# A two-layer hybrid encoder on one Trainium2 core: program unrolled, stages meeting by token halves, five weight slots, norm roots on ScalarE, new mixer order

## The reference

```python
def rms_norm(x, g):
    y = xf * lax.rsqrt(jnp.mean(xf * xf, axis=-1, keepdims=True) + EPS)
    return (y * g.astype(jnp.float32)).astype(x.dtype)

def swiglu(h, w_gate, w_up, w_down):
    return (jax.nn.silu(h @ w_gate) * (h @ w_up)) @ w_down

for l in range(DEPTH):
    h = swiglu(rms_norm(x, ffn1_norm_pre[l]), ffn1_w_gate[l], ffn1_w_up[l], ffn1_w_down[l])
    x = x + 0.5 * rms_norm(h, ffn1_norm_post[l])
    proj = rms_norm(x, mix_norm_pre[l]) @ w_in[l]
    lru_x, lru_g, sq, sk, sv, dq, dk, dv = jnp.split(proj, list(IN_OFFSETS), axis=-1)
    y = jnp.concatenate([y_lru, y_swa, y_diff], axis=-1) @ w_out[l]
    x = x + rms_norm(y, mix_norm_post[l])
    h = swiglu(rms_norm(x, ffn2_norm_pre[l]), ffn2_w_gate[l], ffn2_w_up[l], ffn2_w_down[l])
    x = x + 0.5 * rms_norm(h, ffn2_norm_post[l])
```

## Time and profile before

| | us |
|---|---|
| median of 3 runs | 1081.08 (1079.9 to 1083.06) |
| profiled execution, its own time | 1079.87 |
| its span in the trace | 1078.1 |
| TensorE busy | 1001.6 (93%) |
| VectorE busy | 703.5 (65%) |
| ScalarE busy | 511.8 (47%) |
| GpSimd busy | 112.6 (10%) |
| mean granted TensorE clock | 0.967 |

### The profile page before, as it was taken

The page is one execution under the profiler, slowest core; times in us unless marked ns, Lnnn a source line. Parts: engine busy times, 40 slices in busy tenths (PEclk is TensorE's granted clock), DMA queues, the critical chain, the costliest instruction groups (busy, mean ns, idle before and its releaser), DMA issues. The chain is left out here.

```text
span 1078.1 us, 15592 instructions
## 1 busy us (share of the span) xinstructions
PE 1001.6 (93%) x5486; PEld 865.2 (80%) x5486; DVE 703.5 (65%) x895; ACT 511.8 (47%) x646; POOL 112.6 (10%) x84
## 2 busy tenths in 40 slices
PE   7999999699994999999879999996999959999996
PEld 6888888588984888888768888885889758888885
DVE  6765556757778666556677655667577776655655
ACT  5444444345563544444354444443456535444442
POOL 5000000304004000000130000003130130000000
PEclk9999999889997999999989999998999969999998
DMA  8767656423342556556355655563342525565550
GB/s 235 251 212 263 194 178 232 135 90 127 136 147 88 159 192 195 188 191 209 116 139 194 195 190 191 172 226 117 117 138 100 167 75 187 193 195 177 177 171 40
DMA packets 131246, 180.57 MB, mean 167 GB/s; under 512 B 4112, under 2 KB 114840, under 8 KB 131200
## 3 DMA queue, kind: packets, MB, share of 16 engines
q1 hardware_dynamic: 128944, 176.24, 49.7%
q0 software_dynamic: 2256, 3.76, 1.7%
HBM read 178.92 MB, written 2.63 MB: 168 GB/s over the span
## 5 line engine op out<-in xcount | busy, mean ns | idle before, releaser
L458 PE MATMUL UP<-xT,whi 128*128 128x512 f32 x1648 | 582.6, 398 | 4.9 <-DVE xT L1052 4.9
L997 DVE TENSOR_TENSOR wlo<-raw,whi 128x2048 fp32r<-128x2048 f32 (+1 forms) x156 | 355.3, 2280 | 185.7 <-ACT whi L739 185.5
L460 PE MATMUL UP<-xT,wlo 128*128 128x256 f32 x1648 | 461.9, 280 | 0.0
L458 PEld LDWEIGHTS UP<-xT,whi 128*128 128x128 f32 x1648 | 309.4, 188 | 80.6 <-issue 6.3
L739 ACT ACTIVATE whi<-raw 128x2048 fp32r<-128x2048 f32 x162 | 306.0, 1891 | 131.2 <-PE Y L481 125.2
L460 PEld LDWEIGHTS UP<-xT,wlo 128*128 128x128 f32 x1648 | 311.2, 189 | 1.4
L481 PE MATMUL Y<-whi,hidT 128*128 128x512 f32 x640 | 178.9, 391 | 0.0
L481 PEld LDWEIGHTS Y<-whi,hidT 128*128 128x128 f32 x640 | 117.4, 188 | 24.6
L506 PE MATMUL UP<-ident 128*128 128x128 f32 x276 | 50.5, 357 | 54.1 <-DVE x L1070 29.3
L481 PE MATMUL Y<-wlo,hidT 128*128 128x512 f32 x320 | 99.5, 392 | 0.0
L506 PEld LDWEIGHTS UP<-ident 128*128 128x128 f32 x276 | 47.4, 265 | 58.3 <-DVE x L1070 30.7
(11 more groups left out here) (182 smaller groups left out, 828.8 us busy)
## 6 DMA issues: line engine op xcount, KB each, us to landing
raw<-in_ffn_w_gate SPq DMA_DIRECT2D x44, 1024.0 KB, 5.4
raw<-in_ffn_w_up SPq DMA_DIRECT2D x44, 1024.0 KB, 5.4
raw<-in_ffn_w_down SPq DMA_DIRECT2D x44, 1024.0 KB, 4.8
raw<-in_w_in SPq DMA_DIRECT2D x20, 1024.0 KB, 5.1
raw<-in_w_out SPq DMA_DIRECT2D x6, 1024.0 KB, 4.8
gains<-in_ffn_norm_pre SPq DMA_DIRECT2D x4, 512.0 KB, 4.8
gains<-in_ffn_norm_post SPq DMA_DIRECT2D x4, 512.0 KB, 5.4
raw<-in_w_out SPq DMA_DIRECT2D x4, 512.0 KB, 3.6
```

The costliest lines, as they stand in the source:

```text
L458: nc.tensor.matmul(dst[:, 0:2 * S], h[:, kt, c:c + P], xT[:, kt, :, :].rearrange("p h s -> p (h s)"), start=kt == 0, stop=False, skip_grou ...
L460: mm = nc.tensor.matmul(dst[:, S:2 * S], o[:, kt, c:c + P], xT[:, kt, 0, :], start=False, stop=kt == KT - 1, skip_group_check=True)
L997: V.tensor_tensor(wlo[:, slot, 0:n], raw[:, slot, 0:n], whi[:, slot, 0:n].bitcast(F32), ALU.subtract).then_inc(lo_ready, 1)
```

## The change

The whole program is unrolled: no loops on any engine.

*Ring.* Five slots. `wlo` is laid over `raw`, so the low part of a unit is written in place over what was loaded. A unit is loaded when PE has used the unit five before (`unit_used`), and split at the same condition. All weight splits are on ACT and DVE.

*Feed-forward order.* The down unit of pair i follows the up unit of pair i + 2 (`LAG`), and the last three down units stand at the end (`TAIL`): first their token half 0, then their half 1. Hidden values lie in four places of `yT`.

*Stage boundary.* Norms, additions and transposes go by token half `t` and feature half `h`. DVE does `post` and `pre` for half 0 and then for half 1, POOL none of it. The root of a norm is an ACT square root (`norm_root`) followed by a reciprocal and one refinement on DVE (`norm_scale`); `load_root_table` calls Sqrt once at the end of each feed-forward stage. PE turns the first quarter of the next stage before the last six matmuls of a feed-forward stage (after them in a mixer), and begins the next stage with two units in which tokens are rows (`token_units`): for both units the products with the high part of `x`, then those with the low part, first for half 0 and then for half 1. They are gate and up of pair 0, whose hidden values are turned by four more transposes, or in a mixer the two value units. Between the halves PE runs 3 + 3 identity matmuls.

*Mixer.* Order new, four output units of two row blocks each instead of three such and two single ones; the two value units first, window attention last of the three jobs.

*Start and end.* The first `x` half is loaded first; the 28 identity matmuls before the first transposes are gone. The output is stored in four pieces.

The core of the diff:

```diff
-RING = 3
...
+RING = 5
...
+for pair_ in range(PAIRS):
+    FFN_ORDER += [("gate", pair_), ("up", pair_)]
+    if LAG <= pair_ < PAIRS - 1:
+        FFN_ORDER.append(("down", pair_ - LAG))
+TAIL = tuple(range(PAIRS - 1 - LAG, PAIRS))
+FFN_ORDER += [("down", pair_) for pair_ in TAIL]
...
+        wlo = nc.alloc_sbuf_tensor_at("wlo", [P, RING, 2048], F32R, offset=ring_base)
         whi = sb("whi", [P, RING, 2048], F32R)
-        wlo = sb("wlo", [P, RING, 2048], F32R)
...
+                if k >= RING:
+                    sp.wait_ge(unit_used, k - RING + 1)
+                sp.dma_start(dst, src).then_inc(raw_loaded[k % RING], 16)
...
-                split(l, FFN2_0)
-                add_first(l * 3 + 1)
-                weigh_first(l * 3 + 2)
...
-            def turn_x(stage):
-                for t in range(NT):
-                    pe.wait_ge(x_ready[t], stage + 1)
-                    keep_clock(4)
-                pe.wait_ge(x_squared, stage * 3 + 3)
-                keep_clock(6)
-                for h, t in TURN_ORDER:
-                    if h == 0:
-                        pe.wait_ge(xs_ready[t], stage + 1)
...
+            def turn(s, t, h):
+                pe.wait_ge(xs_ready, quarter(s, t, h) + 1)
+                for kt in range(4 * h, 4 * h + 4):
+                    tr = nc.tensor.transpose(UP[:, 1024 * t + P * kt:1024 * t + P * kt + P],
+                                             xs[:, t, kt * P:(kt + 1) * P], ident[:, :])
+                tr.then_inc(xs_turned, 1)
...
+            def token_units(s, t, first_signal):
+                units = stage_unit(s, 0), stage_unit(s, 1)
+                tok = slice(t * P, t * P + P)
+                for n, k in enumerate(units):
+                    unit_ready(k)
+                    for kt in range(KT):
+                        if n == 0 and kt % 4 == 0:
+                            pe.wait_ge(xT_hi, quarter(s, t, kt // 4) + 1)
+                        dst = bank(Y, 2 * t + n, 0, UC)
+                        nc.tensor.matmul(dst, xT[:, kt, 0, tok], cols(k, whi)[:, kt, :], start=kt == 0, stop=False)
+                        nc.tensor.matmul(dst, xT[:, kt, 0, tok], cols(k, wlo)[:, kt, :], start=False, stop=False)
+                for n, k in enumerate(units):
+                    for kt in range(KT):
+                        if n == 0 and kt % 4 == 0:
+                            pe.wait_ge(xT_lo, quarter(s, t, kt // 4) + 1)
+                        mm = nc.tensor.matmul(bank(Y, 2 * t + n, 0, UC), xT[:, kt, 1, tok], cols(k, whi)[:, kt, :],
+                                              start=False, stop=kt == KT - 1)
+                    mm.then_inc(unit_used if t else first_signal, 1)
+            def enter(s, first_signal, turned_parts):
+                for h in range(turned_parts, 2):
+                    turn(s, 0, h)
+                token_units(s, 0, first_signal)
+                if s:
+                    pe.wait_ge(x_half, quarter(s - 1, 1, 0) + 1)
+                    keep_clock(3)
+                    pe.wait_ge(x_squared, quarter(s, 1, 1) + 1)
+                    keep_clock(3)
+                for h in range(2):
+                    turn(s, 1, h)
+                token_units(s, 1, first_signal)
...
+                        for b in range(2):
+                            token_rows(k, hidden_parts(i), 0, b, False, True).then_inc(y_banks, 1)
+                for i in TAIL:
+                    k = ffn_unit(s, "down", i)
+                    if i < TAIL[-1]:
+                        both_banks(k, hidden_parts(i), 1).then_inc(unit_used, 1)
+                    else:
+                        token_rows(k, hidden_parts(i), 1, 0, False, True).then_inc(y_banks, 1)
+                        if s + 1 < STAGES:
+                            turn(s + 1, 0, 0)
+                        token_rows(k, hidden_parts(i), 1, 1, False, True).then_inc(unit_used, 1)
...
+            def norm_root(s, t, kind):
...
+                A.activation(root[:, t, kind:kind + 1], ss[:, t, kind, 1:2], ACT.Sqrt, scale=1.0 / (D * factor * factor),
+                             bias=base_sum[:, t, kind:kind + 1]).then_inc(root_ready, 1)
...
+            def load_root_table():
+                act.wait_ge(eps_set, 1)
+                A.activation(nw[:, 3, 3:4], epsb[:, :], ACT.Sqrt)
...
+                for t in range(NT):
+                    if s:
+                        square_y(s, t, 0)
+                        if t:
+                            turned_hi(s, 0, 1)
+                        square_y(s, t, 1)
+                        norm_root(s, t, POST)
+                        if t == 0:
+                            for k in splits:
+                                split(k)
+                    for h in range(2):
+                        square_x(s, t, h)
...
+                V.scalar_tensor_tensor(half, ss[:, t, kind, 1:2], -0.5 / (D * factor * factor), half_sum[:, t, kind, 0:1], ALU.mult, ALU.add)
+                dve.wait_ge(root_ready, root_number(s, t, kind) + 1)
+                link(V.reciprocal(y, root[:, t, kind:kind + 1]))
+                link(V.scalar_tensor_tensor(w, y, half, y, ALU.mult, ALU.mult))
+                link(V.scalar_tensor_tensor(y, w, 1.5, y, ALU.add, ALU.mult))
...
+            def post(s, t, between=lambda: None):
+                weigh_y(s, t, 0)
+                norm_base(s, t, POST)
...
+                weigh_y(s, t, 1)
+                norm_scale(s, t, POST)
+                for h in range(2):
+                    add_y(s, t, h)
+            def pre(s, t):
+                norm_base(s, t, PRE)
+                norm_scale(s, t, PRE)
+                for h in range(2):
+                    weigh_x(s, t, h)
+            def enter(s, splits):
+                if s:
+                    post(s, 0)
+                    for k in splits:
+                        split(k)
+                    pre(s, 0)
+                    post(s, 1, lambda: turned_lo(s, 0, 0))
+                    turned_lo(s, 0, 1)
+                    pre(s, 1)
...
+                in_tile(U_SWKV, 0)
+                turn_output(l, JOB_A)
+                in_tile(U_SWKV, 1)
+                pe.wait_ge(mix_lo, l * OUT_UNITS + 1)
+                turn_weights(l, JOB_B)
+                scores(l, JOB_SWA)
+                in_tile(U_LRU_G, 0)
+                values(l, JOB_B)
+                lru_gate(l, 0)
+                in_tile(U_LRU_G, 1)
+                lru_gate(l, 1)
...
+                both_banks(out_unit(OUT_A), mixed(OUT_A), 0, True)
+                wait_tile_read(pe, l, U_LRU_G, 1)
+                turn_output(l, JOB_B)
...
+                job_output(JOB_A)
+                tile(U_SWQ, 1)
+                softmax_weights(JOB_B)
+                tile(U_SWKV, 0)
+                job_lo(JOB_A, 1)
+                sp(11)
+                softmax_logits(JOB_SWA)
+                tile(U_LRU_G, 0)
+                sp(12)
+                job_output(JOB_B)
+                tile(U_LRU_G, 1)
+                softmax_weights(JOB_SWA)
+                recurrence_inputs()
+                job_lo(JOB_B, 2)
```

More of the change, by code:

```diff
@@ L974, in _ @@
[L974 to L985 removed]
+                A.activation(sm[:, 8, 0:2], sm[:, 7, 0:2], ACT.Exp, scale=-1.0)
@@ new lines, in small_parameters @@
+                A.activation(sm[:, 0, 4:6], sm[:, 0, 0:2], ACT.Exp).then_inc(sp_exp, 1)
+            load_root_table()
+            for s in range(STAGES):
+                enter(s, [stage_unit(s, 1)] if s and s % 3 != 2 else [])
+                if s % 3 == 1:
+                    mixer(s)
+                else:
+                    ffn(s)
+            for t in range(NT):
+                for b in range(2):
+                    square_y(STAGES, t, b)
+                norm_root(STAGES, t, POST)
@@ L1367, in shape_constants @@
+            for t in range(NT):
+                post(STAGES, t)
 def shape_constants():
```

1540 lines of the change are left out of this document (762 added, 778 removed).

## The result

| | before | after | after / before |
|---|---|---|---|
| median, us | 1080.87 (1079.9 to 1083.06, 4 runs) | 1041.24 (1040.54 to 1042.69, 4 runs) | 0.9632, 95% interval 0.9614 to 0.965 |
| profiled execution, own time, us | 1079.87 | 1041.41 | |
| its span, us | 1078.1 | 1039.6 | |

The account below looks back on a forecast made before the run. PE was taken to bound the kernel, busy 1001.6 of 1078.1 us, with DVE and ACT setting the time only at boundaries, start and end. -46.1 - 38.0 + 1.7 + 4.3 - 4.1 + 6.4 = -75.8 gave 1005.3 us, range 983 to 1038.

Parts of the forecast that it names:

- Boundaries: Between stages: beginning the next stage by token halves saves 46.1 us after three feed-forward stages, 38.0 us after two mixers.
- start: Program start: the third unit comes at 34.5 us where it came at 30.2, costing +4.3 us.
- end: Program end: a chain of 3.8 us replaces GpSimd's 2.34 us steps beside DVE, saving 4.1 us.
- where the two units go: Feed-forward stages: pair 0 with tokens as rows needs four more PE transposes, 0.43 us in each of four, +1.7 us.
- The mixer: Both mixers: DVE takes GpSimd's splits in one queue; waits of 8.2 us where 5 stood, +3.2 each, +6.4 us.
- walking that queue with the durations of the rows: Mixer: adding single DVE step times from the profile to find PE's waits, 8.2 us in all per mixer.
- The clock: Rival: the clock falls to 1.2 GHz at the boundaries, 5.8 to 6.8 us more each, 1037 us; 22 in 100.
- 5 us of the 100.2 are waits now: Mixer before the change: matmuls were counted as 78.2 plus 17 us, leaving 5 us as PE waits.
- late weights: Rival, the case that ends slower: units wait for weights, 1160 us at 1 us each, 1098 at 0.6; 3 in 100.
- a circle of slots: Weight ring: a slot is loaded, split and used in a circle of 5 units, 27.9 us, leaving 12.8 us of cover.
- The boundaries do overlap: Against the rival that half 1's chain starts only after half 0's on ACT and DVE, 1050 us; 5 in 100.
- The tables: Feed-forward stages: 13 ACT table loads for 6, 1.28 us each, the root's load hidden, no extra drain at a switch.

Follow-up runs that it names:

- best2_bare: Changed kernel with the convolution's first two multiplications early, the rest after job B's weights, splits later, and no identity matmuls in the boundaries: 1005.32 us.
- conv_cut: Changed kernel with GpSimd's convolution cut to its first multiplication, three taps and the bias left out: 1014.43 us.
- keep24: Changed kernel with 24 identity calls (48 instructions) on PE in front of the wait for job A's att: 1022.24 us.
- ring4: Changed kernel with four weight slots in place of five: 1137.37 us, 1.051 of before.
- no_overlap20: Changed kernel with half 0's token units moved behind the chain of half 1 and 20 identity calls in their old place: 1059.55 us.
- conv_dve: Changed kernel with the convolution done by DVE in eight fused 256-column steps before the window attention's logits: 1025.50 us.
- split_later: Changed kernel with the weight split before job A's job_output moved behind it and behind job B's softmax_weights: 1037.45 us.
- conv_mid: Changed kernel with GpSimd's convolution started only after the low part of job A's output: 1024.20 us.
- conv_dve_order: As conv_dve, with three of DVE's weight splits one place later as well: 1020.21 us.
- best1: Changed kernel with GpSimd's convolution mostly after job B's weights, four DVE splits one place later, and identity calls at the start: 1020.46 us.

## Why the prediction was wrong

The direction was right, and so was the account of the boundaries; the account of the mixer was wrong. The time, 1041 us, lay 3 us above the range's end, and 36 above the forecast. By its own steps:

| step | forecast, us | measured, us |
|---|---|---|
| third unit of the first stage | 34.5 | 34.65 |
| first stage, third unit to last matmul (173.1 + 1.1 + 0.45 + 0.43) | 175.1 | 175.15 |
| same, second and third stage | 175.1 | 176.68, 175.69 |
| last matmul to third unit, behind feed-forward, three | 14.8 | 15.4 |
| same, behind a mixer, two | 16.5 | 17.8 |
| end, behind the last matmul | 6.9 | 6.18 |
| mixer without value units, two | 92.2 | 108.3, 107.9 |

*Boundaries, start, end, where the two units go: right* within 1.6 us each. Together they gave 76.7 us (38.5 in all and 38.2 that the two mixers took over 89.0) where the sum had 82.2 (-46.1 -38.0 +1.7 +4.3 -4.1). The 5.5 us between are small misses: 12 identity instructions between the halves, which I had not counted and whose removal shortens each of the five boundaries by 0.9 us (best2_bare), and in the second feed-forward stage a wait of 0.85 us for `gate`. Part of the start is luck: the first unit's matmuls began at 18.75 us, and not at 16.8, and the third unit was on time all the same.

*The mixer: the term that failed.* The sum had +3.2 us for each mixer, with an upper bound of +10; it was +19. The step was "walking that queue with the durations of the rows". I took `job_output` at 4.4 us from a row in which GpSimd is idle, without asking where GpSimd's convolution goes when the input units change their order. It came 17 us later than before (261.4 instead of 244.6) and met exactly the small steps that it blocks, which then took 6.66 us and not 3.30 to the first `att` step. What it does to such steps was in my own rows (2.33 us beside the addition), and I used it only for the boundaries. The trace of before has the convolution at 245 us beside splits; comparing both orders on POOL as well as on DVE would have shown it. conv_cut is the proof: without the convolution beside that queue the kernel takes 26.8 us less. The other 9.1 of the 36 us are the 5.5 above, 2.5 by which the two mixers of conv_cut (93.0 and 93.9) exceed 92.2, and 1 that no row settles.

*The clock: the right rival at the wrong place.* I priced a fall at 1037 us in the boundaries, where none came (1.00 in all five), and none in the mixer, where a forecast wait of 2.0 us seemed harmless. It became 6.2 us, and the fall cost 19.0 of the 36 us (keep24). That the price resembles the measured time is chance.

*Errors that cancelled.* The waits that I walked add up to 9.1 us as listed (2.0 + 2.6 + 2.5 + twice 0.5 + 1.0), and not to 8.2. "5 us of the 100.2 are waits now" was wrong: the earlier trace rows has PE busy for 99.61 of 100.37. And of those new waits conv_cut has 4.2 us (93.01 - 88.83): the low part of `yT` and job B's output kept PE from nothing, since the window-value tile, 48 narrow matmuls, covers them. That the mixer without the convolution is 93.0 us, where I had 92.2, is luck.

*The other rivals.* No waits for late weights came; a circle of slots that is too small does make the kernel slower than before (ring4), for the most part at a stage's end and behind it. The boundaries do overlap (no_overlap20). The tables behave as forecast, 13 loads of 1.28 us, each with the next step within 0.02 us, as here:

```profile
539.58 1.28 ACT L812 ACT_TABLE_LOAD   x1
540.88 0.38 ACT L812 ACTIVATE tanh<-Y 128x256 f32<-128x256 f32 x1
```

Open is why the clock fell in one mixer of conv_dve behind a wait of 1.4 us and not in the other. Open too is why a single run of conv_cut took 1022.24 us where three took 1013.4 to 1014.9; its mean granted clock was 0.990 where theirs was 0.999, so part of it ran at the lower clock, but where isn't on record.

## What to carry to other kernels

When an order changes, look up for every engine what now runs beside each critical chain, above all GpSimd's steps beside small DVE steps in SBUF: a chain of twelve 0.16 us steps took twice its time here. Put GpSimd's work beside DVE steps that read the sums, or beside reductions. Price each wait of PE twice, once as idle time and once with half the clock for what stands behind it; identity matmuls that fill most of a long wait bought the second part back here, but count their instructions: where they outlast the wait, they delay the work behind it.

## What the runs showed of the hardware

- Behind the wait of 6.23 us PE was busy for all of 21.92 us, and the granted clock stayed at 0.50. Half of that stretch were 128-column matmuls (48 of the window-value tile, 10.3 us); it rose again among the 512- and 256-column ones of the next tile.
- The mixer is fragile. The lower clock followed waits of 3.92 us (split_later), 3.91 (conv_mid) and 3.33 (conv_dve_order), and also waits of 1.41 (conv_dve, first mixer) and 1.45 (best1): in these last two PE had been at work again for about 2 us when it fell. Behind waits of 1.38 to 1.54 us in conv_cut it didn't fall. Nor did it in the boundaries of the changed kernel, with idle times up to 1.3 us and 256-column matmuls between them. So the length of the wait alone doesn't tell; what else decides is open.
- A DVE step blocked by GpSimd loses up to the length of one GpSimd instruction (1.04 to 1.29 us), whatever its own length, so in these rows the loss depends on the number of steps and not on their work.
